# RWKV scan: the two last products of an item's preparation share two PSUM banks, and their copies come behind both

## The reference, cut to what matters

```
def step(S, inp):
    r_t, w_t, k_t, v_t, kk_t, a_t = inp
    sa = -jnp.einsum('nhvk,nhk->nhv', S, kk_t)
    S = S * w_t[:, :, None, :] + sa[..., None] * (kk_t * a_t)[:, :, None, :] + v_t[..., None] * k_t[:, :, None, :]
    return S, jnp.einsum('nhvk,nhk->nhv', S, r_t)
```

## Time and profile before

| | us |
|---|---|
| median of 3 runs | 4727.53 (4726.03 to 4728.73) |
| time of the profiled execution | 4730.53 |
| its span | 4728.4 |
| busy over the span: PE, DVE, ACT, POOL | 4203.1, 1978.1, 1349.0, 517.5 |
| the scan, about 2860 to 3345 | some 485 |

### The profile page before, as it was taken

How to read it: one execution, slowest core, us unless ns; L and a number is a source line. 1 busy time by engine, 2 the same in 40 slices (tenths; PEclk the granted TensorE clock), 3 DMA queues, 4 the chain that set the end, 5 groups by cost and what they waited for, 6 DMA issues and landing times. The chain is left out here.

```text
span 4728.4 us, 68997 instructions
## 1 busy us (share of the span) xinstructions
PE 4203.1 (89%) x28006; PEld 2447.3 (52%) x28006; DVE 1978.1 (42%) x3941; ACT 1349.0 (29%) x3134; POOL 517.5 (11%) x535
## 2 busy tenths in 40 slices
PE   5999889999998999999997756888698799999994
PEld 2455466644444665355446645767585344443331
DVE  1455256512563664334205665666356222222224
ACT  2125355411244553122113443333132111111110
POOL 0000000000000000000000002222002423222220
PEclk9999999999999999999997877898898899999997
DMA  5122330131323203313011012000304678999995
GB/s 192 52 72 71 119 111 18 63 115 34 97 78 117 91 18 136 143 59 97 28 65 45 2 35 82 3 3 3 116 1 155 236 251 289 320 317 334 333 331 154
DMA packets 199188, 565.69 MB, mean 120 GB/s; under 512 B 24449, under 2 KB 115186, under 8 KB 185426
## 3 DMA queue, kind: packets, MB, share of 16 engines
q1 hardware_dynamic: 162450, 441.90, 25.9%
q0 software_dynamic: 36416, 119.29, 9.2%
HBM read 437.02 MB, written 124.11 MB: 119 GB/s over the span
## 5 line engine op out<-in xcount | busy, mean ns | idle before, releaser
L729 PE MATMUL banks<-arena 128*128 128x512 f32 (+1 forms) x2928 | 1124.5, 541 | 9.8 <-ACT arena L584 5.7
L729 PEld LDWEIGHTS banks<-arena 128*128 128x128 f32 x2928 | 556.3, 192 | 537.4 <-issue 498.0
L3269 PE MATMUL banks<-arena 128*32 128x512 f32 (+2 forms) x2896 | 561.0, 595 | 4.2 <-DMA arena<-in_experts 3.4
L1250 PE MATMUL banks<-arena 128*128 128x256 f32 (+1 forms) x1152 | 377.5, 482 | 18.7 <-DMA arena<-y_d 14.4
L3269 PEld LDWEIGHTS banks<-arena 128*32 128x32 f32 (+2 forms) x2896 | 198.4, 130 | 357.8 <-issue 354.1
L1469 PE MATMUL banks<-arena 96*128 96x512 f32 (+1 forms) x800 | 329.2, 546 | 32.4 <-DMA arena<-k_d 19.9
L1520 DVE TENSOR_REDUCE arena<-banks 128x1 f32<-128x512 f32 (+1 forms) x400 | 226.4, 592 | 293.3 <-PE banks L1469 293.3
L1250 PEld LDWEIGHTS banks<-arena 128*128 128x128 f32 x1152 | 222.2, 194 | 165.4 <-issue 145.7
L3288 PE MATMUL banks<-arena 128*32 128x512 f32 (+2 forms) x1448 | 286.4, 595 | 1.7 <-DVE arena L3318 1.2
L3353 ACT ACTIVATE arena<-banks 128x256 f32<-128x256 f32 x79 | 30.5, 385 | 781.3 <-PE banks L3269 781.3
L3236 POOL DMA_INDIRECT r_d<-arena x125 | 181.5, 1452 | 639.2 <-DVE arena L3318 536.1
(11 more groups left out here) (500 smaller groups left out, 5659.5 us busy)
## 6 DMA issues: line engine op xcount, KB each, us to landing
arena<-in_experts SPq DMA_DIRECT2D x64, 3072.0 KB, 13.0
arena<-in_ada_w SPq DMA_DIRECT2D x12, 2048.0 KB, 7.8
arena<-in_w_in SPq DMA_DIRECT2D x23, 1024.0 KB, 5.5
arena<-in_w_mod SPq DMA_DIRECT2D x8, 2048.0 KB, 18.6
arena<-in_w_out SPq DMA_DIRECT2D x6, 2048.0 KB, 11.5
arena<-in_w_in SPq DMA_DIRECT2D x5, 2048.0 KB, 8.6
arena<-in_tokens SPq DMA_DIRECT2D x4, 2048.0 KB, 17.8
arena<-in_w_mod SPq DMA_DIRECT2D x8, 1024.0 KB, 5.0
```

What stands on the lines that cost most here:

```text
L729: i = e.matmul(self.out_of(n), lhs, rhs, start=k == 0, stop=k == KT - 1)
L1250: i = e.matmul(bank(n % 4)[:, 0:nn], w[:, q, :], H[:, q, t0:t0 + nn], start=q == 0, stop=q == KT - 1)
L3269: op = e.matmul(ABK[(q - q0) % 2][rows, :], xT[(q - q0) % 2][:, P * k:P * k + P][:, rows], weights[:, i % SLOTS, 512 * k:512 * k + 512], s ...
```

## The change

`ub` gets no turn in the banks any more. Its matmuls write columns 256 to 511 of the two banks whose first 128 columns `wt` has just written, chunk 0 (rows 0 to 63) in the first bank and chunk 1 (rows 64 to 127) in the second. TensorE does not wait between them, apart from `X1`, which was copied many stages earlier. ScalarE waits for `ub` before all its copies: two of `wt` (as before), and then two of 64x256 in place of one of 128x256. The banks are free behind the last ones. The chain's first product waits for the copies of `wt` under the new name `turned`; its sum with `UB` waits for the last copy.

```diff
-                    give("wt", n, 0), give("wt", n, 1), give("ub", n)
+                    give("wt", n, 0), give("wt", n, 1)
...
             op.then_inc(Tn.hit("wt", n), 1)
-            o = sl.of("ub", n)
-            sl.free(e, Vn, Sn, "ub", n)
             e.wait_ge(*Sn.at("free", "x1", n))
             for h in range(4):
                 hs_ = slice(64 * h, 64 * h + 64)
-                for tp in half:
-                    op = e.matmul(o[tp, hs_], b.TT_[tp, hs_], b.X1[tp, hs_], start=True, stop=True)
+                for c, tp in enumerate(half):
+                    op = e.matmul(sl.of("wt", n, c)[tp, 256 + 64 * h:320 + 64 * h], b.TT_[tp, hs_], b.X1[tp, hs_], start=True, stop=True)
             op.then_inc(Tn.hit("ub", n), 1)
...
-            e.wait_ge(*Tn.at("wt", n))
+            e.wait_ge(*Tn.at("ub", n))
             for c, tp in enumerate(half):
-                e.activation(b.WTv[:, :, tp], sl.of("wt", n, c)[:, 0:P].rearrange("p (g t) -> p g t", g=2), ACT.Copy, scale=-1.0).then_inc(Sn.hit("free", "wt", n, c), 1)
-            e.wait_ge(*Tn.at("ub", n))
-            e.activation(b.UB, sl.of("ub", n)[:, 0:256], ACT.Copy, scale=-1.0).then_inc(Sn.hit("free", "ub", n), 1)
+                e.activation(b.WTv[:, :, tp], sl.of("wt", n, c)[:, 0:P].rearrange("p (g t) -> p g t", g=2), ACT.Copy, scale=-1.0).then_inc(Sn.hit("turned", n, c), 1)
+            for c, tp in enumerate(half):
+                e.activation(b.UB[tp, :], sl.of("wt", n, c)[tp, 256:512], ACT.Copy, scale=-1.0).then_inc(Sn.hit("free", "wt", n, c), 1)
...
-                e.wait_ge(*Sn.at("free", "wt", n, 1))
+                e.wait_ge(*Sn.at("turned", n, 1))
...
-                e.wait_ge(*Sn.at("free", "ub", n))
+                e.wait_ge(*Sn.at("free", "wt", n, 1))
```

## The result

| | before | after |
|---|---|---|
| median of 4 runs | 4728.13 us (4726.03 to 4735.86) | 4682.38 us (4681.25 to 4684.45) |
| ratio | | 0.9901, 95% interval 0.9887 to 0.9915 |
| profiled execution, its span | 4730.53, 4728.4 | 4681.85, 4679.7 |
| first `wt` of the scan (item 0) to the last (item 19) | 2891.96 to 3326.30: 434.3 us | 2888.42 to 3279.33: 390.9 us |

46 us went where 56 were forecast. The profiled executions differ by 48.7 us, and 434.3 - 390.9 = 43.4 of it lie between the first and the last `wt`. Ahead of item 0's `wt` the second execution was 3.5 us early, and behind item 19's it took 1.7 us less, without the change having touched anything there. So 43.4 is the number to explain, and it is to be set against the sum of 55.8. The median, 4682.38, is 0.4 us above the 4664 to 4682 of the forecast itself (A), and within the whole range.

A forecast was written before the change was run, and what follows sets the result against it. The scan was taken as bound by its written order, a chain over TensorE, ScalarE and VectorE. 34.4 (wait) + 21.4 (clock) = 55.8 us off 4730.5 gave 4674.7, 4672 as median; range 4663 to 4697.

The forecast's parts named there:

- the forecast itself (A): In the scan, the wait before `ub` goes and most clock falls with it: 4664 to 4682 us, chance 0.62.
- The wait: TensorE before `ub`: idle for the copy of `wt` goes and `ub` starts 0.30 us behind `wt`, saving 34.4 us.
- ScalarE's copies: ScalarE's copies of `wt` wait for `ub`, whose copy becomes two of 64x256: taken as 0, at most 7.6 us lost.
- the two banks: `ub`'s matmuls writing two banks: no difference expected, bounds -0.22 to +3.9 us per item.
- the turns of the banks: 21 bank uses per item instead of 22 make `lo` and `cum` of item n+3 wait for `ub`'s copies: 0.
- rival D: `ub`'s matmuls into two banks lose their overlap, 4.6 us in place of 0.68: slower, 4772 us, chance 0.03.
- The clock: TensorE's half-rate falls at `ub` in the scan: 26.8 us at stake, 0.8 of it given to the change, 21.4 us.
- What is late next: Stages behind `tt` on VectorE and GpSimdE: none becomes late, so the whole shift passes to `x` and around the period.
- Rival C: L2466 or GpSimdE becomes the next wait; 1 us back per item gives 4713 us, or 4692 without most falls; chance 0.10.
- the falls at other waits (B): TensorE's clock falls as often as before, at other waits, so only 34 us is saved: 4693 us, chance 0.22.
- the forecast's two terms in full: In the scan, the wait's saving plus all 26.8 us of clock falls at stake: 61.2 us.
- The signs that were named: After-trace: `ub` 0.3 to 0.45 us behind `wt`, period 20.8 to 21.2, clock 0.97 or more, 64x256 copies of 0.38.

The follow-up runs named there:

- fill_before: The kernel before, its wait kept, with five 128x128x128 products of constants added between `wt` and `ub`: 4706.93 us.
- masks_early: The changed kernel with GpSimdE's masks for levels three to five of an item written one stage earlier: 4670.15 us.
- wait_back: The changed kernel's banks and split copies, but TensorE again waits for both copies of `wt` before `ub`: 4733.86 us, ratio 1.0001 to before.
- fill_after: The changed kernel, masks unmoved, with three 128x128x128 products of constants behind `tt` of level two, in TensorE's wait before `x`: 4680.17 us.
- pool_reads: masks_early plus a useless GpSimdE product at the mask's old place, reading two operands and writing one: 4689.29 us.
- pool_writes: masks_early plus a useless GpSimdE memset of 128x768 at the mask's old place, which only writes: 4666.86 us.
- masks_around: As masks_early, but the mask of level five waits until VectorE has made the next item's products to be turned: 4668.51 us.

## Why the prediction was right in the mechanism, and its gain 10 to 12 us too large

**The wait.** Right in place and size. `ub` comes 0.28 us behind `wt` (0.34 to 0.35 at items 18 and 19). Summed over items 0 to 18, which lie in the scan, the distance from `wt` to `ub` was 39.8 us and is 5.4: 34.4 less (35.0 over all 20), and the forecast was 34.4. (For item 18 the prediction read 0.82 where the whole trace has 0.92, because its row shows 14 of 16 records; that is worth 0.2 us.) The scans say the same where neither the clock nor the new collision differs: fill_before and masks_early lie 410.4 - 373.9 = 36.6 us apart, and without fill_before's one fall (1.2) and its overrun at item 18 (0.8) that is 34.6.

**ScalarE's copies, the two banks, the turns of the banks.** Each was costed at nothing and is worth nothing: wait_back has all three and is no faster than before, and ScalarE's copies end 0.64 us before `x` does at item 9 and 0.06 behind it at item 2. `ub` took 0.65 us, so rival D is out. The gate behind the scan passed the gain on, within 2 us.

**The clock.** The cause was right (filling the wait instead of removing it makes the falls vanish too), and so was the size at stake: 26.8 worked out, 23.9 measured, 25.9 with the two corrections. The share that I gave to the change was too high: 0.8, 21.4 us. Measured is 25.9 - 10.8 = 15.1, with the 10.8 us of fill_after still lost. It was a chosen share and not one worked out. The reason for 8.0 of the 10.8 was in the next point; the other 2.8 are the fall at item 1.

**"What is late next" is the step that failed.** It looked at GpSimdE's L2555 only as something that others wait for, ending at 3.04 and needed at 3.4, and at VectorE's L2466 only as something that waits, from 2.56 on. Neither was late. But from 2.56 to 3.04 they now ran at the same time, which they had not before, as the earlier trace rows shows: the mask ended at 3102.30, and L2466 came at 3104.69. Moving TensorE's work 2.8 us ahead moved VectorE's products under GpSimdE's reads. So the step that the whole shift passes on around the period had a term at nothing that was worth 14 us: 6.2 by the slower product and 8.0 by the falls behind it. Rival C had the right place, a stage that gives back part of the gain, but as a wait of 1 us and not as a slower instruction. That the time still fell into the range owes something to luck: the 5.4 us that the share of 0.8 held back stood for a doubt about waits that were there before, and the range's upper end was meant for the falls at other waits (B) and for C as a late engine.

**The account**, along a chain of kernels, each step the difference of two scans (so that they add up by construction): before to fill_before, the clock, 23.9 us; on to masks_early, the wait, 36.6; on to fill_after, the slowed product, 6.2 back; on to the changed kernel, its falls, 10.8 back; in all 43.4. (The fall and the overrun in fill_before move 2.0 us from the wait's step to the clock's.) The scan of masks_early is 17.0 us under the changed kernel's. Of these the collision cost 14.2: 6.2 directly, and 8.0 because 0.4 us more of idle in an already thin stretch brought the clock down, from item 7 on at every third item. The pair pool_reads and pool_writes has 15.2 for it. The other 2.8 are the fall at item 1. Without both the gain in the scan is 434.3 - 373.9 = 60.5 us, against 61.2 for the forecast's two terms in full.

**The signs that were named.** From item 5 to item 17 the period of 20.8 to 21.2 came out as 20.96 to 21.28, and 22.2 to 22.7 with a fall; the clock of 0.97 or more as 0.97; the copies of 64x256 as 0.37 to 0.38.

## What to carry to other kernels

A wait that leaves a chain of engines moves all that follows it against the engines that don't wait there. Ask of each neighbour not only whether it is late, but what it will now run beside: VectorE with two operands in SBUF, next to a GpSimdE instruction that reads there, took up to 2.3 times as long (0.95 us against 0.42). And where TensorE's clock falls at a wait, its price can be measured apart from the wait, by filling the wait with work that nobody needs.

## What the runs showed of the hardware that was not expected

- VectorE's product of two 128x256 operands in SBUF took 0.42 us alone. Beside GpSimdE products, L2464 of the changed kernel took 0.77 in the median and 0.93 at most, and L2468 of masks_early took 0.95 every time. Beside a GpSimdE memset of the same length it took 0.42.
- Matmuls of constants in TensorE's idle time paid for themselves: five per item took the clock over the scan from 0.90 to 1.00 and 22 us off the kernel before, with the wait still there.
- A wait of 1.5 to 2.2 us brought a fall at most items before and none at items 0, 2 and 3. After the change, 0.83 + 0.44 + 0.58 us in three pieces brought one at every third item, and 0.40 us less of it brought none at all. The chain's wait of 1.76 us at item 1 was followed by a fall in the changed kernel and by none in masks_early, fill_after, pool_reads, pool_writes and masks_around. What decides between these cases, the runs don't show.
